# Gate and up projections of two feed-forward layers with features on the partitions instead of tokens, without the transposes behind them

## What is computed

```python
def swiglu(h, w_gate, w_up, w_down):          # FFN_HIDDEN = 2816
    return (jax.nn.silu(h @ w_gate) * (h @ w_up)) @ w_down

h = h + swiglu(rmsnorm(h, norm_ffn[i]), ffn_w_gate[i], ffn_w_up[i], ffn_w_down[i])
```

## Time and profile before

| | |
|---|---|
| median of 3 runs | 1014.9 us (1014.52 to 1014.96) |
| the profiled execution's own time | 1015.26 us |
| its span in the profile | 1013.4 us |
| PE busy in the span | 993.4 us (98%) |
| DVE, ACT, POOL busy | 635.6, 506.4, 129.3 us |

### The profile page before, as it was taken

How to read it: one execution, slowest core, us unless ns; L and a number is a source line. 1 busy time by engine, 2 the same in 40 slices (tenths; PEclk the granted TensorE clock), 3 DMA queues, 4 the chain that set the end, 5 groups by cost and what they waited for, 6 DMA issues and landing times.

```text
span 1013.4 us, 14604 instructions
## 1 busy us (share of the span) xinstructions
PE 993.4 (98%) x5869; PEld 865.7 (85%) x5869; DVE 635.6 (63%) x981; ACT 506.4 (50%) x751; POOL 129.3 (13%) x207
## 2 busy tenths in 40 slices
PE   7999999999999999999999999999999999999997
PEld 6889788888888898988888888888989889999995
DVE  6867677555556875555765555568665877555554
ACT  7666745444444655554544444456564355434442
POOL 5000796800000000000000000012500000000000
PEclk9999999999999999999999999999999999999999
DMA  9944469955555564243475555545643337656521
GB/s 277 299 136 143 104 154 209 301 175 199 179 195 177 176 204 145 111 126 125 150 244 178 195 181 193 183 132 195 191 163 110 100 125 253 204 168 205 171 81 42
DMA packets 112724, 174.77 MB, mean 172 GB/s; under 512 B 5977, under 2 KB 73569, under 8 KB 112657
## 3 DMA queue, kind: packets, MB, share of 16 engines
q1 hardware_dynamic: 106224, 165.43, 51.0%
q0 software_dynamic: 6272, 8.15, 3.3%
q10 hardware_dynamic: 160, 0.27, 0.1%
HBM read 172.77 MB, written 1.05 MB: 172 GB/s over the span
## 4 chain that ended last, share of the span: by engine, by line
PE 91%; DVE 5%; ACT 2%; DMA 1%; issue 1%; SPq 0%; DVEq 0%; ACTq 0%
PE bank L1017 27%; PE bank L1019 27%; PE bank L1018 27%; PE bank L1130 2%; DVE wl L1531 1%; PE bank L1160 1%; PE bank L1032 1%; PE bank L1187 1%; DMA raw<-in_da_w_qkv_dram 1%; PE bank L1246 1%; PE bank L1193 1%; PE bank L1180 1%; PE bank L1140 1%; ACT wh L607 1%; PE bank L1163 0%
## 5 line engine op out<-in xcount | busy, mean ns | idle before, releaser
L1531 DVE TENSOR_TENSOR wl<-raw,wh 128x2048 fp32r<-128x2048 f32 x154 | 355.2, 2312 | 185.2 <-ACT wh L607 185.1
L607 ACT ACTIVATE wh<-raw 128x2048 fp32r<-128x2048 f32 x154 | 292.0, 1909 | 118.4 <-PE bank L1019 111.8
L1017 PE MATMUL bank<-wh,xh 128*128 128x512 f32 (+2 forms) x664 | 250.5, 377 | 1.6 <-DVE xl L1608 1.0
L1019 PE MATMUL bank<-wh,xl 128*128 128x512 f32 (+2 forms) x664 | 245.9, 370 | 0.0
L1018 PE MATMUL bank<-wl,xh 128*128 128x512 f32 (+2 forms) x664 | 245.8, 370 | 0.0
L1017 PE MATMUL bank<-xh,wh 128*128 128x256 f32 (+1 forms) x672 | 194.7, 290 | 1.0 <-DVE wl L1847 0.5
L1018 PE MATMUL bank<-xl,wh 128*128 128x256 f32 (+1 forms) x672 | 190.4, 283 | 0.0
L1019 PE MATMUL bank<-xh,wl 128*128 128x256 f32 (+1 forms) x672 | 190.4, 283 | 0.0
L1017 PEld LDWEIGHTS bank<-wh,xh 128*128 128x128 f32 (+1 forms) x664 | 125.2, 189 | 22.6 <-issue 2.0
L1019 PEld LDWEIGHTS bank<-wh,xl 128*128 128x128 f32 (+1 forms) x664 | 125.0, 188 | 22.2
L1018 PEld LDWEIGHTS bank<-wl,xh 128*128 128x128 f32 (+1 forms) x664 | 125.3, 189 | 20.3
(11 more groups left out here) (248 smaller groups left out, 854.4 us busy)
## 6 DMA issues: line engine op xcount, KB each, us to landing
raw<-in_w_ff_dram SPq DMA_DIRECT2D x32, 1024.0 KB, 5.2
raw<-in_ffn_w_gate_dram SPq DMA_DIRECT2D x44, 512.0 KB, 4.0
raw<-in_ffn_w_up_dram SPq DMA_DIRECT2D x44, 512.0 KB, 5.0
raw<-in_ffn_w_down_dram SPq DMA_DIRECT2D x22, 1024.0 KB, 5.0
raw<-in_na_w_qkv_dram SPq DMA_DIRECT2D x12, 1024.0 KB, 5.2
raw<-in_w_in_dram SPq DMA_DIRECT2D x12, 1024.0 KB, 5.2
raw<-in_da_w_qkv_dram SPq DMA_DIRECT2D x11, 1024.0 KB, 11.5
raw<-in_ple_w_gate_dram SPq DMA_DIRECT2D x8, 1024.0 KB, 5.0
```

The lines of the kernel that those rows point to most:

```text
L607: nc.scalar.activation(wh[:, i % RING, :], raw[:, i % RAW, :], ACT.Copy).then_inc(s_hi, 1)
L1017: nc.tensor.matmul(dst, lh, rh, start=start, stop=False, skip_group_check=True)
L1019: return nc.tensor.matmul(dst, ll, rh, start=False, stop=stop, skip_group_check=True)
L1531: nc.vector.tensor_tensor(wl[:, i % RING, :], raw[:, i % RAW, :], wh[:, i % RING, :].bitcast(F32), ALU.subtract).then_inc(s_lo, 1)
```

## The change

In layers 1 and 2 the up product takes `features_unit`'s shape: gate in bank 4 or 6, value in bank 5 or 7, in turn. The gate is multiplied by r, spread along the free dimension, on DVE; ACT takes the tanh of half of it; DVE forms (1 + tanh) x gate and multiplies by the value. The r of the value and the factor one half are put on where the down product is added to the residual (scalar `r_half` per token, L1621's place). The result already has its features on the partitions: the turns (`a_turn`) are gone, ACT copies `ah` from SBUF in one piece of 512 columns and DVE makes `al` in one piece. DVE makes the diagonal behind `late_roots`, PE spreads it into bank 0 behind up(0) and waits until ACT has copied it. The diff, cut to its core (the lists of semaphore keys follow it):

```diff
@@ up product, PE @@
-                def up_2(j, kh):
-                    return features_unit(first["up", 2, j] + kh, kh, pair(4 + 2 * (j % 2)), True, slice(X0, XP), name,
-                                         fine=True, signal=s_up2)
-
                 def up(j, kh):
-                    banks = [up_bank(j, b) for b in range(TB)]
-                    return tokens_unit(first["up", l, j] + kh, kh, banks, name, 0, 1, signal=up_done.sem,
-                                       fine=(j, kh) == (0, 0))
+                    return features_unit(first["up", l, j] + kh, kh, pair(4 + 2 * (j % 2)), True, slice(X0, XP), name,
+                                         fine=True, signal=s_up2 if l == 2 else up_done.sem)
...
-                for b in range(TB):
-                    wait(pe, added, f"wo{l}", 0, b)
-                first_unit(up(0, 0), name, (1, 4))
+                first_unit(up(0, 0), name, (1, 2))
                 run(up(0, 1))
+                for c in range(2):
+                    for b in range(TB):
+                        wait(pe, added, f"wo{l}", c, b)
+                spread_root(name, bank[0])
+                wait(pe, r_ready, name)
                 for j in range(1, n_it + 1):
                     if j < n_it:
                         if j >= 2:
-                            for b in range(TB):
-                                wait(pe, act_a, l, j - 1, b)
+                            wait(pe, act_a, l, j - 2, 0)
                         run(up(j, 0))
-                        if j == 1:
-                            for b in range(TB):
-                                a_turn(0, b)
                         run(up(j, 1))
...
+                    wait(pe, a_lo, l, j - 1, 0)
                     for at, (b, k, n) in enumerate(parts):
...
-                            if j < n_it and d == dn - 1 and at % 4 == 3:
-                                a_turn(j, b)
@@ feed_forward, ScalarE @@
+                    if j == 0:
+                        spread_root(name, bank[0])
+                    wait(act, gated, l, j)
+                    nc.scalar.activation(e_s[:, 1, :], e_s[:, 0, :], ACT.Tanh, scale=0.5).then_inc(act_e.sem, 1)
                     split_to(u + 2 + (dn if j else 0) + 3)
...
+                    wait(act, act_a, l, j, 0)
+                    if j >= 1:
+                        used(act, first["down", l, j - 1])
+                    nc.scalar.activation(ah[:, 0:512], a_s[:, 0, :], ACT.Copy).then_inc(a_hi.sem, 1)
@@ feed_forward, VectorE @@
                         turns_lo(name, 1)
-                        late_roots(name, EPS if l < 2 else EPS_2, 0.5 if l < 2 else 1.0)
+                        late_roots(name, EPS if l < 2 else EPS_2, 1.0)
+                        if l < 2:
+                            at = 2 * NORMS.index(name)
+                            diagonal(name, rstd[:, at:at + 2])
                     split_to(u + 2 + (1 if j == 0 else 3))
...
+                    if j == 0:
+                        wait(dve, r_ready, name)
+                    wait(dve, up_done, l, j, 1)
+                    gate, value = bank[4 + 2 * (j % 2)], bank[5 + 2 * (j % 2)]
...
+                    nc.vector.tensor_tensor(e_s[:, 0, :].rearrange("p (g s) -> p g s", g=2),
+                                            gate[:, :].rearrange("p (g s) -> p g s", g=2),
+                                            r_cols[:, META:T].unsqueeze(1).to_broadcast([P, 2, S]),
+                                            ALU.mult).then_inc(gated.sem, 1)
+                    wait(dve, act_e, l, j, 0)
+                    link(nc.vector.scalar_tensor_tensor(out=a_s[:, 1, :], in0=e_s[:, 1, :], scalar=1.0, in1=e_s[:, 0, :],
+                                                        op0=ALU.add, op1=ALU.mult))
+                    used(dve, u + 1)
+                    nc.vector.tensor_tensor(a_s[:, 0, :], a_s[:, 1, :], value[:, :], ALU.mult).then_inc(act_a.sem, 1)
                     split_to(u + 2 + (dn if j else 0) + 3)
...
+                    wait(dve, a_hi, l, j, 0)
+                    nc.vector.tensor_tensor(al[:, 0:512], a_s[:, 0, :], ah[:, 0:512].bitcast(F32),
+                                            ALU.subtract).then_inc(a_lo.sem, 1)
@@ add_scale, VectorE @@
-                        nc.vector.tensor_tensor(h[half], h[half], bank[2 * b + n][:, :], ALU.add).then_inc(added.sem, 1)
+                        if stage in ("dn0", "dn1"):
+                            nc.vector.scalar_tensor_tensor(out=h[half], in0=bank[2 * b + n][:, :],
+                                                           scalar=r_half[:, LATER.index("ffn" + stage[-1]), b:b + 1],
+                                                           in1=h[half], op0=ALU.mult, op1=ALU.add).then_inc(added.sem, 1)
...
@@ GpSimd @@
-            wait(pool, act_a, 1, ffn_shape[1][0] - 1, 1)
+            wait(pool, act_a, 1, ffn_shape[1][0] - 1, 0)
```

More of the change, by code:

```diff
@@ L255, in two_blocks_kernel @@
         ATT = [(l, i) for l in range(3) for i in range(16)]
-        ITS = [(l, j, b) for l in range(3) for j in range(ffn_shape[l][0]) for b in range(2)]
+        ITS = [(l, j, b) for l in range(3) for j in range(ffn_shape[l][0]) for b in range(1 if l < 2 else 2)]
         s_raw = [sem(f"raw_landed{i}") for i in range(RAW)]
@@ L311, in two_blocks_kernel @@
         added = Order(sem("added"), RES)
[L312 removed]
+        up_done = Order(sem("up_done"), [(l, j, m) for l in range(2) for j in range(ffn_shape[l][0]) for m in range(3)])
+        gated = Order(sem("gate_over_rms"), [(l, j) for l in range(2) for j in range(ffn_shape[l][0])])
         act_e = Order(sem("act_e"), ITS)
         act_a = Order(sem("act_a"), ITS)
[L315 removed]
         a_hi = Order(sem("a_hi"), ITS)
@@ new lines, in feed_forward @@
+                    w_hi, w_lo = (w.rearrange("p (k n) -> p k n", k=2) for w in unit(first["down", l, j - 1]))
+                    last = j == n_it
+                    parts = [(b, k, n) for b in range(TB) for k in range(2) for n in range(2)]
+                    if last:
+                        parts = [(b, k, n) for n in range(2) for b in range(TB) for k in range(2)]
+                    wait(pe, a_lo, l, j - 1, 0)
+                    for at, (b, k, n) in enumerate(parts):
+                        cols = slice(S * k + b * P, S * k + (b + 1) * P)
+                        ins = three(bank[2 * b + n][:, :], (ah[:, cols], al[:, cols]),
+                                    (w_hi[:, k, 512 * n:512 * n + 512], w_lo[:, k, 512 * n:512 * n + 512]),
+                                    j == 1 and k == 0, last and k == 1)
+                        if at == 7:
+                            ins.then_inc(s_used, 1)
+                        elif last and k == 1:
+                            ins.then_inc(summed.sem, 1)
@@ L1799, in feed_forward @@
                         continue
[L1800 to L1805, removed]
-                            nc.vector.scalar_tensor_tensor(out=a_s[:, b, 0:256], in0=e_s[:, b, 256:512],
-                                                           scalar=r_sq[:, i_, b:b + 1], in1=up_bank(j, b)[:, 256:512],
-                                                           op0=ALU.mult, op1=ALU.mult).then_inc(act_a.sem, 1)
```

42 lines of the change are left out of this document (8 added, 34 removed).

## The result

The changed kernel takes **1025.2 us** (median of 4 runs, 1024.31 to 1025.47) against 1014.93 us of the kernel before in runs beside it (4 runs, 1014.52 to 1015.57): a ratio of 1.0099, with an interval of 1.0083 to 1.0115. It is slower by 10.3 us. The profiled execution took 1025.47 us, with a span of 1023.6.

What follows compares the result with a forecast made beforehand. PE was taken to bound the kernel, busy 98% of the span. Terms 3.1 + 2.5 + 3.7 + 0.6 = 9.9 us on the profiled 1015.26 gave 1025.2; with the runs' median 0.36 lower, 1024.8 us, range 1021 to 1029.

Steps and rivals of the forecast that it cites:

- A: Steady step of layers 1 and 2: 16.97 us instead of 16.83, so +3.1 us over both layers.
- B: Behind up(0), PE spreads the root and waits for ACT's copy: 1.25 us later per layer, twice +2.5 us.
- C: Between down(9) and down(10), PE waits for ah and al written in one piece: 1.83 us, twice +3.7 us.
- D: Between up(0)'s two units, PE waits for the residual's second half, xl: 0.32 us, twice +0.6 us.
- the lower bounds of B and C: Least cost per layer: 0.5 us for the spread's two passes alone, 0.6 with only ACT late in the last step.
- the rival of hidden waits: Waits behind up(0) and ahead of down(10) fall to their lower bounds: 5.9 us slower, about 1020 us; chance 7%.
- the turns give nothing back: Rival for the steps of layers 1 and 2: removing transposes saves nothing, +10.8 us on top, 1035.6 us; chance 2%.
- DVE late in the first step: Rival: DVE's chain behind the spread exceeds its 0.8 us cover (or is late in the last step): 1029.4 us; chance 9%.
- about 13 ns of each matmul don't depend on its columns: Reading of block 3's rows: two 256-column halves take 240 ns, one 512-column whole 227.
- Back-to-back issue gap: Rule pricing the up product's halves at 109.2 ns: only 2.7 us more, sum -0.8; lies in a rival given 4%.

Runs made afterwards that it cites:

- e5_no_turns: Kernel before the change, with the transposes of the product left out, so the result lacks them: 1003.91 us, ratio 0.9889.
- e2_no_pe_wait: Changed kernel without PE's wait for ACT's copy of the spread root: 1023.35 us.
- e1_halves: Changed kernel with ah and al written per token block again, the first piece waiting only for the first half of the down product before: 1021.71 us.
- e3_turns_earlier: Changed kernel with the residual's second half turned one column block earlier in up(0)'s first unit: 1025.26 us, one run.
- e8_192_half_block: Changed kernel, up product of layers 1 and 2 with 64 instead of 128 stationary columns and 192 of 256 tokens, the rest left out: 961.95 us.
- e7_wide_pair: Changed kernel plus e1_halves, e2_no_pe_wait, e3_turns_earlier; in steps 2 to 10 two matmuls of each triple merged into one of 512 columns: 1017.39 us, ratio 1.0023.

## Why the prediction was right, and the one reading that was not

The prediction was 1024.8 us and slower; it came out at 1025.2. By its own parts, for one layer where not said otherwise:

| part | predicted | measured | shown by |
|---|---|---|---|
| A, the step | 16.97 us | 16.98 us | timeline after; the turns' share by `e5_no_turns` |
| B, the spread | 1.25 us | 1.18 us | timeline after; the layer is 0.70 shorter in `e2_no_pe_wait` |
| C, the last step | 1.83 us | 1.83 us | timeline after; the layer is 1.87 shorter in `e1_halves` |
| D, the first unit | 0.32 us | 0.32 us | timeline after; the layer is 0.33 shorter in `e3_turns_earlier` |
| sum of two layers | 9.9 us | 9.86 us | 2 x (190.95 - 186.02) |

**A** was right because block 3 already had the new shape in the same program, so that its rows were a price and not an estimate. **B** came out 0.07 lower, by readings that differ both ways: PE went on 0.05 us behind ACT's copy where the prediction took the 0.14 that it had read behind a DVE result, and the first matmul took 0.11 longer and not 0.08. **C** was right because rows 8 show the same chain over ACT and DVE, and because the prediction asked at which step nothing stands between the copy and its reader. That the total agrees to 0.4 us is in part luck: the start of up(0) alone moves by more than that from one execution to another. That the lower bounds of B and C would hold (the rival of hidden waits) fell with the holes; that the turns give nothing back fell with `e5_no_turns`, which measured 11.0 us for them against 10.8 predicted. DVE late in the first step didn't happen, by the margin of 0.8 us that was foreseen, and `e8_192_half_block` shows that the mechanism exists.

**The reading that was off** is a sentence of the first part: "about 13 ns of each matmul don't depend on its columns". The number that it stood for is right (two halves 240 ns, one whole 227), and so is the sum that rests on it. The explanation isn't. With the half block, 256 columns take 113.4 ns and 512 take 229.6 (5.51 us over 24), so that two halves cost no more than one whole; with the whole block, 512 columns take the same 227, but 256 take 120, and 192 take 111.4 where the half block takes 88.6. So a stream of 512 columns covers what the stationary block costs, and one of 256 no longer does quite: 6.5 ns a matmul stick out. Whether at 256 columns these are the load itself or also the half block's fewer partitions of output, no run separates. On 2112 matmuls they are 13.7 us, about the 13.4 by which the prediction raised part A; by this sum the turns' 10.8 us would without it have been gained nearly in full in the steady steps. What a column costs where the block doesn't matter stays open too: with the half block 0.39 ns from 192 to 256 columns and 0.45 from 256 to 512. The floor could have been read before the change, from the 112 ns of L1494.

The floor is near what loading the block would make. The Trainium skill, page "TensorE: Matmul & The Clock Gate", section "LDWEIGHTS (loading the stationary operand)", gives the time of a load in ns as the stationary columns over 1.2, which for 128 is an estimate of 107 ns from that page. The traces' 112 ns at 2 streamed columns and 111.4 at 192 lie within 5 ns of it. The section "Back-to-back issue gap" of the same page of the Trainium skill, whose formula the prediction weighed as a rival, would have the halves at 109 ns and the wholes at 216, an estimate from that page; it calls the formula that of an isolated matmul. The traces have 120 and 227 with a new block for each matmul, and 113.4 and 227 at best.

No version beats the kernel before. The best that does the whole computation, `e7_wide_pair`, is 2.5 us behind the runs beside it. Two ways were not tried, and no run tells whether they are possible: a second buffer for `ah` and `al`, and adding the two products of `e7_wide_pair` up in the same 256 columns.

## What to carry to other kernels

Where a change gives one stage a shape that another stage of the same kernel has already, read the price of the shape from there before counting what is removed: here the transposes were worth 11.0 us, and the two halves in place of one whole cost some 14 (a step of 16.98 us against the 16.32 of `e5_no_turns`, 22 steps). Exchanging the stationary and the streamed operand can double the number of stationary blocks to be loaded; what that costs depended here on how many columns are streamed over each. And of a buffer that is now written in one piece, ask at the first and the last step what still stands between its writer and its reader.

## What the hardware showed that was not expected

Start-to-start distances of float32 matmuls with a new stationary block each, at a granted clock of 1.00:

| streamed columns | block of 128 columns | block of 64 columns |
|---|---|---|
| 2 (L1494 of the kernel before) | 112 ns | not measured |
| 192 | 111.4 ns | 88.6 ns |
| 256 | 120 ns | 113.4 ns |
| 512 | 227.3 ns | 229.6 ns |

The column of the whole block is flat up to 192 streamed columns and then no straight line: 256 columns are past the floor of 111.4 and still take 6.5 ns more than with the half block. And a narrow matmul between two wide ones doesn't get its own price: 512 and 256 columns in turn take 353 ns together (`e7_wide_pair`), 6 more than 227 and 120.
